# Two-stage attention block on one core: a shallower attention pipeline, 64-row low-half products, packed indexer queries and a reordered low-rank norm

## The reference

```python
# block 1: 8 "fox" heads (forget-gate attention) and 8 "nsa" heads (3 gated branches)
s = einsum('bhqd,bkhd->bhqk', q, k) * SCALE + c_q - c_k            # fox, causal
s = einsum('bgrqd,bgkd->bgrqk', q, k) * SCALE + bias               # nsa: selected, window, compressed
p = masked_softmax(s, mask);  o = p @ v
# block 2: 16 meta tokens in front; heads A (sliding window 128, sinks), heads B (latent, indexed)
iq, ik: 4 indexer heads of 64;  score = sum_h relu(iq_h @ ik.T) * iw_h      # per query
sel = top_k(score, 128)                                            # per query, only these keys count
q = rms_norm(bq, q_norm_g) @ w_uq                                  # bq: rank 256
o_a = sliding_window_sink_attention(aq, ak, av, sinks)
o_b = softmax(q_abs @ c_kv[sel] * scale + bias) @ c_kv[sel]
```

## Time and profile before

| what | us |
|---|---|
| median of 3 runs | 1693.24 |
| lowest, highest | 1692.65, 1703.56 |
| the profiled execution, device time | 1703.56 |
| its span, first to last instruction | 1701.8 |
| mean granted TensorE clock | 0.945 |

### The profile page before, as it was taken

How to read it: one execution, slowest core, us unless ns; L and a number is a source line. 1 busy time by engine, 2 the same in 40 slices (tenths; PEclk the granted TensorE clock), 3 DMA queues, 4 the chain that set the end, 5 groups by cost and what they waited for, 6 DMA issues and landing times.

```text
span 1701.8 us, 19427 instructions
## 1 busy us (share of the span) xinstructions
PE 1581.7 (93%) x7174; PEld 1255.3 (74%) x7178; DVE 828.4 (49%) x1588; ACT 616.0 (36%) x1132; POOL 359.2 (21%) x434
## 2 busy tenths in 40 slices
PE   6899988899999999999998877779999999999995
PEld 5787665588877888888886755448887788888884
DVE  5446554444444333433458796334444443443444
ACT  5433455522234222322454455433223322222222
POOL 3200643400020000000136346540002120120112
PEclk9899778999999999999999877789999999999998
DMA  5734100233322333333324600022332233333321
GB/s 188 131 90 129 57 1 13 66 107 99 99 84 77 99 97 91 97 100 99 94 87 110 114 13 1 7 87 87 99 100 87 87 97 92 96 99 99 100 78 59
DMA packets 41918, 145.47 MB, mean 85 GB/s; under 512 B 5170, under 2 KB 5362, under 8 KB 41824
## 3 DMA queue, kind: packets, MB, share of 16 engines
q1 hardware_dynamic: 37088, 128.98, 24.4%
q0 software_dynamic: 4736, 15.25, 4.4%
HBM read 138.32 MB, written 5.36 MB: 84 GB/s over the span
## 4 chain that ended last, share of the span: by engine, by line
PE 83%; DVE 8%; ACT 4%; issue 3%; DMA 1%; POOL 1%; DVEq 0%; SPq 0%; ACTq 0%; POOLq 0%
PE PSA L494 81%; PE PSA L659 2%; ACT AR L1119 1%; PE PSA L789 1%; DVE AR L1553 1%; DVE AR L1551 1%; DVE WL L1463 1%; DMA WR<-w_in 0%; DVE AR L1969 0%; DVE ARR L1559 0%; DVE PSA L1501 0%; DVE AR L1666 0%; ACT AR L1130 0%; ACT AR L1169 0%; DVE AR L1578 0%
## 5 line engine op out<-in xcount | busy, mean ns | idle before, releaser
L494 PE MATMUL PSA<-Ah,WH 128*128 128x512 f32 x1072 | 430.3, 401 | 21.7 <-DVE WL L1463 21.7
L494 PE MATMUL PSA<-Al,WH 128*128 128x512 f32 x1072 | 424.0, 395 | 0.0
L494 PE MATMUL PSA<-Ah,WL 128*128 128x512 f32 x1072 | 423.6, 395 | 0.0
L1047 ACT CAST WH<-WR 128x1024 fp32r<-128x1024 f32 (+3 forms) x233 | 239.7, 1032 | 237.1 <-PE PSA L494 236.0
L1463 DVE TENSOR_TENSOR WL<-WR,WH 128x1024 fp32r<-128x1024 f32 (+3 forms) x223 | 269.4, 1209 | 97.6 <-ACT WH L1047 97.3
L494 PEld LDWEIGHTS PSA<-Ah,WH 128*128 128x128 f32 x1072 | 205.4, 192 | 69.1 <-issue 22.7
L494 PEld LDWEIGHTS PSA<-Ah,WL 128*128 128x128 f32 x1072 | 205.3, 191 | 43.9
L494 PEld LDWEIGHTS PSA<-Al,WH 128*128 128x128 f32 x1072 | 205.5, 192 | 43.0 <-issue 0.7
L494 PE MATMUL PSA<-Bh,WH 128*128 128x512 f32 x584 | 226.6, 388 | 2.2 <-DVE ARR L1559 2.2
L494 PE MATMUL PSA<-Bh,WL 128*128 128x512 f32 x584 | 226.5, 388 | 0.0
L494 PE MATMUL PSA<-Bl,WH 128*128 128x512 f32 x576 | 224.1, 389 | 0.0
(11 more groups left out here) (357 smaller groups left out, 2010.5 us busy)
## 6 DMA issues: line engine op xcount, KB each, us to landing
WR<-w_in SPq DMA_DIRECT2D x228, 512.0 KB, 3.5
WR<-w_in SPq DMA_DIRECT2D x8, 384.0 KB, 3.1
XT<-scr_tmp POOLq DMA_DIRECT2D x8, 264.0 KB, 12.8
XT<-xT_in SPq DMA_DIRECT2D x4, 512.0 KB, 8.4
XT<-scr_tmp POOLq DMA_DIRECT2D x8, 256.0 KB, 13.4
XT<-xT_in POOLq DMA_DIRECT2D x1, 2048.0 KB, 10.1
x_tmp<-XT POOLq DMA_DIRECT2D x1, 2048.0 KB, 9.0
XT<-x_tmp POOLq DMA_DIRECT2D x1, 2048.0 KB, 9.3
```

The costliest lines, as they stand in the source:

```text
L494: return pe.matmul(o, l, r, start=start, stop=stop)
L1047: ac.copy(WH[p][:, 0:n], WR[j % RAW][:, 0:n]).then_inc(w_hi, 1)
```

## The change

1. D_T, D_V go from 6, 8 to 4, 6, in both attentions.
2. In nsa and A scores the key's low part is multiplied with 64 rows, both heads of a pair behind both 128-row products.
3. IQ has two heads in 128 rows (no zeros, no POOL memsets, two DVE instructions less), and the index products have 64 rows.
4. The nq norm moves forward: sums before `aq` 0, spread behind `aq` 0; ACT's root directly behind the squares; DVE's variance and Newton step before `aq` 0, the low halves one tile earlier.
5. Top-k steps are spread anew: 4 and 6 become 2 and 2 around `nk`; 19 in the `aq` loop become 20 (with 2 more before it), with more of them behind the q splits; the 8 in the `uq` loop go. In all 11 fewer before attention2 (64 are left for it, not 53).

```diff
-        IQ, IK = v3(8192, 4, 512), AR[:, 5248:5776]
+        IQ, IK = v3(4224, 2, 512), AR[:, 5248:5776]
-        D_T, D_V = 6, 8
+        D_T, D_V = 4, 6
@@ scores1
-                    if x == "f":
-                        mm(o[w], QF[h][:, q0:q0 + 128], KF[h][:, 0:n], True, False)
-                    else:
-                        kh, kl = (KSH, KSL) if br == 1 else (KWH, KWL)
-                        mm(o[w], QN[h][:, q0:q0 + 128], kh[h // 4][:, 0:n], True, False)
-                        mm(o[w], QN[h][:, q0:q0 + 128], kl[h // 4][:, 0:n], False, True).then_inc(p_sc, 1)
+                    k = KF[h] if x == "f" else (KSH if br == 1 else KWH)[h // 4]
+                    mm(o[w], (QF if x == "f" else QN)[h][:, q0:q0 + 128], k[:, 0:n], True, False)
+                for w in range(2):
+                    h, r = h0 + w, hrows(h0 + w)
+                    k = KFL[h // 2] if x == "f" else (KSL if br == 1 else KWL)[h // 4]
+                    last = mm(o[w], (QF if x == "f" else QN)[h][r, q0:q0 + 128], k[r, 0:n], False, x == "n")
@@ scores2, heads A
-                        mm(o[w][:, meta:n], q[w], KAL[g][:, k0:k0 + n - meta], False, True).then_inc(r_sc, 1)
+                        mm(o[w][:, meta:n], q[w][r, :], KAL[h // 4][r, k0:k0 + n - meta], False, True).then_inc(r_sc, 1)
@@ PE, index products
-                    last = mm(PSF[:, b * 512 + c0:b * 512 + c1], IQ[:, h, 128 * qt:128 * qt + 128], IK[:, c0:c1], True, True)
+                    last = mm(PSF[:, b * 512 + c0:b * 512 + c1], IQ[hb:hb + 64, h // 2, 128 * qt:128 * qt + 128],
+                              IK[hb:hb + 64, c0:c1], True, True)
@@ PE, norm nq
             low_rank_spread("nk", TM)
+            pe.wait_ge(v_g.sem, v_g.end("nk"))
+            low_rank_sums("nq", NT2, T)
             for i, b in enumerate((4, 5, 0, 1)):
...
                 if i == 0:
-                    pe.wait_ge(v_g.sem, v_g.end("nk"))
-                    low_rank_sums("nq", NT2, T)
-                if i == 1:
                     low_rank_spread("nq", T)
@@ ACT
                 low_rank_square("nq", k, bqr[:, k, :], NT2, T)
+            low_rank_root("nq", T)
...
-                if i == 0:
-                    low_rank_root("nq", T)
-                if i == 2:
+                if i == 1:
@@ DVE
-            for h in range(2):
-                r = hrows(h)
-                dv.tensor_tensor(IQ[r, h, :], bank(1)[r, :], rb[r, 0:T], ALU.mult).then_inc(i_iq, 1)
+            dv.tensor_tensor(IQ[:, 0, :], bank(1), rb[:, 0:T], ALU.mult).then_inc(i_iq, 1)
...
-            top_run(4)
+            top_run(2)
             low_rank_newton("nk", TM)
-            top_run(6)
+            top_run(2)
...
+            low_rank_var("nq", 256.0, T)
+            top_run(2)
+            low_rank_newton("nq", T)
             for i, b in enumerate((4, 5, 0, 1)):
                 result(tid["aq", i])
                 scaled(bank(b), rb[:, 0:T])
...
+                top_run(2)
+                dv.wait_ge(h_hi.sem, h_hi.at("aq", 2 * i + 1))
+                q_low(h_lo, QA, i, b, 0.125)
...
+                top_run((4, 2, 4, 2)[i])
             for i in range(4):
-                top_run(2)
                 dv.wait_ge(h_hi.sem, h_hi.at("uq", 2 * i + 1))
@@ POOL
-            pl.memset(IQ[64:128, 0:4:2, :], 0.0).then_inc(i_qz, 1)
-            pl.memset(IQ[0:64, 1:4:2, :], 0.0).then_inc(i_qz, 1)
```

More of the change, by code:

```diff
@@ L353, in build @@
         u_hi, u_lo, u_ad = sem("u_hi"), sem("u_lo"), sem("u_ad")
-        i_iq, i_qz = sem("i_iq"), sem("i_qz")
+        i_iq = sem("i_iq")
         i_bg, i_ln, i_lr, i_tr, i_sc, i_re, i_dv = (sem("i_bg"), sem("i_ln"), sem("i_lr"), sem("i_tr"), sem("i_sc"),
@@ L634, in scores1 @@
                         pe.wait_ge(p_mx, i + w - 3)
-                    if x == "f":
-                        mm(o[w], QF[h][:, q0:q0 + 128], KF[h][:, 0:n], True, False)
-                    else:
-                        kh, kl = (KSH, KSL) if br == 1 else (KWH, KWL)
-                        mm(o[w], QN[h][:, q0:q0 + 128], kh[h // 4][:, 0:n], True, False)
-                        mm(o[w], QN[h][:, q0:q0 + 128], kl[h // 4][:, 0:n], False, True).then_inc(p_sc, 1)
+                    k = KF[h] if x == "f" else (KSH if br == 1 else KWH)[h // 4]
[4 more added lines that the diff above has]
+                    last = mm(o[w], (QF if x == "f" else QN)[h][r, q0:q0 + 128], k[r, 0:n], False, x == "n")
+                    if x == "n":
+                        last.then_inc(p_sc, 1)
                 if x == "f":
-                    for w in range(2):
-                        h, r = h0 + w, hrows(h0 + w)
-                        mm(o[w], QF[h][r, q0:q0 + 128], KFL[h // 2][r, 0:n], False, False)
                     for w in range(2):
@@ L763, in scores2 @@
                             mm(o[w][:, c0:c1], q[w], KBA[:, h0 + w, c0:c1], True, False)
-                if x == "B":
-                    for w in range(2):
-                        h, r = h0 + w, hrows(h0 + w)
+                for w in range(2):
+                    h, r = h0 + w, hrows(h0 + w)
+                    if x == "A":
+                        mm(o[w][:, meta:n], q[w][r, :], KAL[h // 4][r, k0:k0 + n - meta], False, True).then_inc(r_sc, 1)
+                    else:
                         for c0, c1 in parts2(n):
                             mm(o[w][:, c0:c1], q[w][r, :], KBLA[r, h // 2, c0:c1], False, False)
+                if x == "B":
                     for w in range(2):
@@ L928, in tensor_program @@
             pe.wait_ge(i_ln, 12)
-            pe.wait_ge(i_iq, 4)
-            pe.wait_ge(i_qz, 2)
+            pe.wait_ge(i_iq, 2)
             for a in range(5):
@@ L937, in tensor_program @@
             for n, (qt, h) in enumerate(index_of):
-                w, b = SCw[qt], 2 + 2 * (n % 2)
+                w, b, hb = SCw[qt], 2 + 2 * (n % 2), 64 * (h % 2)
                 if n > 1:
@@ L1947, in vector_program @@
             result(tid["iq", 1])
-            for h in range(2, 4):
-                r = hrows(h)
-                dv.tensor_tensor(IQ[r, h, :], bank(0)[r, :], rb[r, 0:T], ALU.mult).then_inc(i_iq, 1)
+            dv.tensor_tensor(IQ[:, 1, :], bank(0), rb[:, 0:T], ALU.mult).then_inc(i_iq, 1)
             result(tid["bkv", 0])
@@ L2183, in pool_program @@
             pl.memset(AVM, 0.0).then_inc(h_z, 1)
-            pl.wait_ge(n_ps.sem, n_ps.end("nx"))
-            pl.memset(IQ[64:128, 0:4:2, :], 0.0).then_inc(i_qz, 1)
-            pl.memset(IQ[0:64, 1:4:2, :], 0.0).then_inc(i_qz, 1)
-            pl.wait_ge(i_qz, 2)
             weights_low(tid["bkv", 0])
```

7 lines of the change are left out of this document (removed).

## The result

The changed kernel takes 1715.8 us (median of 6 runs, 1711.0 to 1717.4) against 1693.3 for the kernel before: the ratio is 1.011, with an interval from 1.008 to 1.014. It is slower by 22.5 us, where I had forecast 4.5 us less. The profiled execution has a span of 1712.6 us.

The account below looks back on a forecast made before the run. Groups f were taken as bound by PE at a half-slow clock, the other attention groups by a loop through all engines. Terms summed to -4.5 us from the 1693.24 median, about 1689; range 1674 to 1702.

Parts of the forecast that it names:

- depth, all of it: Shallower pipeline in both attentions: -7 in groups n, 0 in f, +2 and +2.8 at the ends, -3.5 in attention2.
- 64-row scores: Score products of groups n and A: pairs run at once but borders cost time; 0 in all, bounds -3 and +3.
- indexer: Index products: DVE and POOL savings covered, stretch set by DVE's sums and top-k steps; 0, bounds -1 and +3.
- norm: Sums of nq before aq 0: new 5.9 us stall, partly made up behind it; +1.2, bounds -3.5 and +5.
- my step (3.1): DVE's chain before attention2: 7 fewer top-k steps give 3.5 us, of which 0.4 returns as a wait for ACT.
- the 3 to 4 that I named as a sign: PE's wait before attention2, expected to be still some 3 to 4 us if the forecast held.
- The end of attention1: Last values but one to the last: the last pair's whole chain is open, 3.3 us become 5.2; +2.
- the mask: Attention2, from A to B: mask open for 1.6 us but refill narrower, 14.6 us and not 15.7; -1.1.
- The end of attention2: Last step of attention2, with the meta keys' transposes: 3.7 us become 6.5; +2.8.
- clock rival: In attention, PE waiting less is granted 2.4 GHz for longer: -10 to -20 on top, 1668 to 1679; chance 0.22.
- too-shallow pipeline: Transposes before each values block wait for a chain longer than four steps: 1699, 1706 or at worst 1713; chance 0.2.
- depth does nothing: ACT's sum per cycle is unchanged and the 1.0 us gain comes back elsewhere: 1693 to 1697; chance 0.18.

Follow-up runs that it names:

- second profile of before: The kernel before, unchanged, profiled once more because its first profiled execution was 10 us above its median: 1692.8 us, profiled span 1694.0.
- first profile of before: The kernel before, unchanged, in the profiled execution that the prediction was read from: 1703.56 us, the slowest of three and 10.3 above their median.

## Why the prediction was wrong, point by point

**Which term failed.** I forecast -4.5 us and measured +22.5. By parts, each from the runs above:

| part | forecast | measured |
|---|---|---|
| depth, all of it | -5.7 | -10.1 |
| 64-row scores | 0 | +12.2 |
| indexer | 0 | +15.9 |
| norm | +1.2 | +8.6 |

They add up to 26.6, 4 more than the whole. The norm makes this difference: on top of the depth and the 64-row scores it costs 5.0 (1699.9 for 1694.9) and not 8.6. The two terms that I had put at 0 make most of the error, 28.1 us, and the norm 4 to 7; the depth gave 4.4 of it back.

**Indexer: the step that failed.** I wrote that the index products "lie in a stretch that DVE's sums and top-k steps set", with bounds of -1 and +3. True for the kernel before. I reckoned a 64-row product to cost the same as one over 128 rows at the same clock, plus a border, and never asked what the clock does when the zeros go. It costs 15.8 us, all in that one stretch. The 128-row product with half its rows zero was no waste, as PE time there is free.

**64-row scores: the step that failed.** The border that I read from the rows, 0.09 to 0.10, was fair. A cycle of n with both kernels at 2.4 GHz shows it (each pair of scores, and behind the first two the transposes that follow). With the depth alone:

```profile
293.46 1.19 PE L494 MATMUL PSA<-ARR,WL 128*128 128x512 f32 x4
294.49 0.72 PE L659 MATMUL PSA<-CST,AR 128*128 128x128 f32 x4
294.96 0.94 PE L494 MATMUL PSA<-ARR,WL 128*128 128x384 f32 x4
295.74 0.27 PE L659 MATMUL PSA<-CST,AR 128*128 128x128 f32 x1
...
296.49 0.72 PE L494 MATMUL PSA<-ARR,WL 128*128 128x256 f32 x4
```

and in the changed kernel, whose last two of each four are over 64 rows:

```profile
296.45 1.14 PE L493 MATMUL PSA<-ARR,WL 128*128 128x512 f32 x4
297.52 0.68 PE L657 MATMUL PSA<-CST,AR 128*128 128x128 f32 x4
297.96 0.96 PE L493 MATMUL PSA<-ARR,WL 128*128 128x384 f32 x4
298.85 0.33 PE L657 MATMUL PSA<-CST,AR 128*128 128x128 f32 x1
...
299.63 0.79 PE L493 MATMUL PSA<-ARR,WL 128*128 128x256 f32 x4
```

From its start to that of the transposes, as I had measured it in the prediction, the pair takes 1.07 us and not 1.03 at 512 keys, and 0.89 and not 0.78 at 384. From values to values this cycle takes 8.96 us and not 8.64: 0.3 a group, near the +0.2 that I had, but it does not lie under ACT; the cycle is longer by it. In the seven cycles of n that is 1 to 2 us. The larger part of the cost in n is the clock (0.92 to 0.95 in place of 0.98, and 1.7 us in the last values). In A the clock of the first cycles is lower too (0.62 in place of 0.75 or more), and how much time that costs is open. In my list of rivals the clock stood as one that could only gain; its "against" line said that 64-row products leave less in the array, and I gave that no price and no case of its own on the slow side.
The Trainium skill, TensorE: Matmul & The Clock Gate, Part 1, ties the clock to how busy TensorE has lately been. The measurement differs: PE was busy for 48.67 of 49.50 us in the index products and had 0.50 throughout. The measurement decides. The Trainium skill, TensorEngine Tiling (Array Packing), Tiling Modes, which I had weighed in the prediction, says that tiles run independently; the trace agrees where two different halves stand side by side (1.26 us for two of 1.15), and that page says nothing of the clock.

**Norm: the term mis-sized.** The stall is as forecast (5.9, measured 5.62 in the changed kernel and 6.01 alone), and the gap before the spread is gone. What I left out is the clock after a stall of 6 us, 3.6 us. DVE's chain became shorter by about the amount of my step (3.1): from 982.61 to 1006.27 it was 23.7 us, and from 996.84 to 1017.70 it is 20.9. Of the changed kernel, the sums (before: the earlier trace rows) and the start of attention2 (before: the earlier trace rows):

```profile
965.90 3.54 PE L493 MATMUL PSA<-ONE,AR 128*128 128x1 f32 x16 [5.62 <-ACT AR L1085]
```

```profile
1017.70 0.55 PE L493 MATMUL PSA<-Bh 128*128 128x256 f32 x1 [8.26 <-DVE ARR L2020]
```

PE's wait before attention2 is 8.26 us, not the 3 to 4 that I named as a sign. DVE's chain did shrink, by 2.8 us, but PE's own stretch beside it shrank more, from 16.6 to 12.6 us; the wait is the difference of the two, and my sign took PE's part as fixed.

**Depth: right in its mechanism, too small.** The cycles of n gain 8.6 us where the sum had 7 (7.7 to 6.6 a cycle was the forecast; among the last cycles long and short ones take turns, and from the end of the values to the next ones the short go from 7.0 to 6.3, the long from about 10 to 8.5). On top come 2.9 us in the values, which run at 2.4 GHz but for one block, and 1.6 in f, which I had at 0. The end of attention1 costs 1.0 and not 2. The first fill of attention2 gains 2 us as forecast. Attention2 from its first to its last values lasts 103.5 to 107.7 us in the four kernels with the depth and with A's products unchanged, for 107.1 to 109.4 in those without it. The gain lies in its second half: from the last values of A to the last of B it takes 60.4 to 61.1 us with the depth, and 64.3 to 66.6 without it, where I had put 1.1 on the mask and 0.5 on each cycle of B. In A, where I had 1.1 more, it takes 42.9 to 47.3 us, and 42.3 to 44.3 without the depth.
The end of attention2 was priced right and its consequence missed. The last step (before: the earlier trace rows, from 1130.22 to 1133.96) takes 6.9 us in the changed kernel, from 1135.30, behind the output product of the last values but one, to 1142.16, where I had 6.5. But behind this longer wait the last values run at half clock. The second profile of before, and the changed kernel:

```profile
1127.23 2.37 PE L494 MATMUL PSA<-AR 128*64 128x512 f32 x16
```

```profile
1142.16 4.54 PE L493 MATMUL PSA<-AR 128*64 128x512 f32 x16
1146.63 1.27 PE L493 MATMUL PSA<-WW,AR 64*128 64x512 f32 x2
...
1150.87 0.76 PE L493 MATMUL PSA<-Ah,WH 128*128 128x512 f32 x1 [2.97 <-DVE WL L1460]
```

From the meta keys' product to the end of the values it is 5.5 us in place of 2.9. This is most of the 3 to 4 us by which the rest is longer in every kernel with the depth in attention2; in the changed kernel some of what is left lies at 1330 to 1335 us, where the granted clock is 0.66, and 1.00 at the same place in the second profile of before.

**The rivals.** The clock rival (faster) was half right: with the depth alone the clock in n does rise, from 0.90 to 0.98, and this is a good part of the gain beyond my sum. The same clock, in the other direction, is most of what made the change slow. I had also sized it wrongly: at levels of 1.2 and 2.4 GHz a mean of 0.79 is 0.42 of the time at the lower one and 0.95 is 0.10, so a share of 0.32 would change its level, not 0.16, and the rival's gain could have been twice as large. The too-shallow pipeline did not slow the kernel at 4 and 6; its sign, PE waiting for POOL, is 0.2 us at most in n, and in attention2 it is there (13.3 us for 7.2) without making it longer. That depth does nothing is refuted. No case of mine held what happened, and so the range ended at 1702.

**What stays open.** The "dense" stage is 3.6 us longer in the changed kernel. Of this 1.7 are the last values of attention1 at a lower clock, and 1.6 lie at about 500 us, where after the same wait as in all kernels the clock falls for some us in some profiles and not in others. All five profiles with 64-row scores in pairs show it, but so do the first profile of before and two of the kernels with full rows. I can't say whether it is chance. What the 5 us of the 64-row scores in A consist of is open as well, and so is why 64-row products one at a time keep the clock down; the runs show only that they do. The runs of one kernel differ mainly in the mean clock: the ten of the depth alone go from 1677.7 us at 0.961 to 1689.0 at 0.951.

## What to carry to other kernels

Price each edit of TensorE's work twice, once at the clock that it has now and once for what it does to the clock. Before taking zero rows out of a product, see whether another product fills the other half of the array at the same time; one at a time, 64-row products held it at 1.2 GHz here for 50 us although TensorE was idle for less than 1 us of them, and the same products in pairs did not. And ask for every new stall of several us what runs behind it: the 6 us before the sums cost 9.6 before anything was made up.

The version that beats both kernels is the depth alone: 1682.7 us for 1692.8 before and 1715.8 with the whole change.

## What the runs showed of the hardware that I had not expected

- TensorE busy for 48.7 of 49.5 us, with 64-row fp32 products one at a time between 128-row weight products, stayed at 1.2 GHz for the whole 49.5 us. With zeros in the other 64 rows it returned to 2.4 GHz 3 to 7 us after the first product (ten profiles), and with the two halves side by side after 3.5 and 3.8 (two profiles).
- Zeros cost nothing here: the index products before had half of their rows zero, and their stretch took 33.8 us with them, as with the 64-row products in pairs, and 49.5 with the 64-row products one at a time.
- Two 64-row products on different halves take 1.26 us together where one over 128 rows takes 1.15.
- Two steps less in the pipeline's depth turn a gain of 10 us (4 and 6) into a loss of 79 us (2 and 4).
